# Banded values a step later in one row with scores and flips, warm-up matmuls at the start, and the last tile in halves

## The reference, cut to what matters

```python
hn = rmsnorm(x, norm_g[l])
proj = hn @ w_in[l]                       # 1024 -> 3072
u, g_main, q_mem, g_mem = jnp.split(proj, [D_MAIN, 2 * D_MAIN, 2 * D_MAIN + D_MEMW], axis=-1)
if l < N_A:   # layer 0: causal conv and RG-LRU recurrence on u
    y = rglru(causal_conv(u, ...))
else:         # layer 1: rope(u) are the queries of a sliding-window attention with sinks
    y = sink_attend(rope(u), k_att, v_att, band_mask, sinks)   # 16 heads, window 128
om = mem_attend(q_mem, mem_k[l], mem_v[l])                     # 4 heads, 256 memory rows
z = concat([y * silu(g_main), om * silu(g_mem)])
x = x + z @ w_out[l]                      # 1536 -> 1024
```

## Time and profile before

| what | value |
|---|---|
| three runs | 2111.63 to 2113.28 us, median 2112.22 us |
| the profiled execution's own time | 2113.13 us |
| its span | 2111.3 us |
| TensorE matmuls busy | 2087.1 us, 99% |
| VectorE busy | 1148.6 us, 54% |
| ScalarE busy | 923.7 us, 44% |
| granted TensorE clock over the span | 0.999 |

### The profile page before, as it was taken

The page is one execution under the profiler, slowest core; times in us unless marked ns, Lnnn a source line. Parts: engine busy times, 40 slices in busy tenths (PEclk is TensorE's granted clock), DMA queues, the critical chain, the costliest instruction groups (busy, mean ns, idle before and its releaser), DMA issues.

```text
span 2111.3 us, 29268 instructions
## 1 busy us (share of the span) xinstructions
PE 2087.1 (99%) x11869; PEld 1676.5 (79%) x11869; DVE 1148.6 (54%) x2015; ACT 923.7 (44%) x2012; POOL 26.8 (1%) x30
## 2 busy tenths in 40 slices
PE   7999999999999999999999999999999999999998
PEld 6888887777777788788788888888888888787886
DVE  4845446777776822221635444676777777723232
ACT  5733335777777723222534333444434445422111
POOL 0000000000000000000400000000000000000000
PEclk9999999999999999999999999999999999999999
DMA  9311111111111465343111111212222214475353
GB/s 388 127 63 45 63 49 54 45 50 44 44 49 63 164 214 180 107 125 101 61 43 43 36 43 48 78 52 79 69 71 78 68 54 135 132 269 188 89 192 104
DMA packets 116159, 206.28 MB, mean 98 GB/s; under 512 B 12349, under 2 KB 66941, under 8 KB 111025
## 3 DMA queue, kind: packets, MB, share of 16 engines
q1 hardware_dynamic: 116024, 204.42, 28.9%
HBM read 155.97 MB, written 48.48 MB: 97 GB/s over the span
## 4 chain that ended last, share of the span: by engine, by line
PE 92%; DVE 5%; ACT 2%; DMA 1%; issue 0%; SPq 0%; DVEq 0%
PE bank L569 49%; PE bank L1993 23%; PE bank L414 3%; PE bank L1132 3%; PE bank L674 2%; PE bank L1121 2%; PE bank L867 1%; PE bank L661 1%; PE bank L1102 1%; PE bank L649 1%; PE bank L589 1%; DVE wo_lo L1729 1%; PE bank L664 1%; PE bank L1981 1%; PE bank L1445 0%; DMA sm_rows<-srow_scratch 0%
## 5 line engine op out<-in xcount | busy, mean ns | idle before, releaser
L569 PE MATMUL bank<-x_hi,w_hi 128*128 128x512 f32 x1600 | 636.2, 398 | 1.2 <-ACT it_kraw L619 1.2
L569 PE MATMUL bank<-x_hi,w_lo 128*128 128x512 f32 x1600 | 624.1, 390 | 0.0
L569 PE MATMUL bank<-x_lo,w_hi 128*128 128x512 f32 x1600 | 623.3, 390 | 0.0
L569 PEld LDWEIGHTS bank<-x_hi,w_hi 128*128 128x128 f32 x1600 | 300.2, 188 | 100.7 <-issue 39.4
L569 PEld LDWEIGHTS bank<-x_hi,w_lo 128*128 128x128 f32 x1600 | 300.3, 188 | 64.4
L569 PEld LDWEIGHTS bank<-x_lo,w_hi 128*128 128x128 f32 x1600 | 300.5, 188 | 60.7 <-issue 0.7
L1993 PE MATMUL bank<-wo_hi,z_hi 128*128 128x512 f32 x768 | 303.1, 395 | 2.1 <-DVE z_lo L1758 2.1
L1993 PE MATMUL bank<-wo_hi,z_lo 128*128 128x512 f32 x768 | 299.2, 390 | 0.0
L1993 PE MATMUL bank<-wo_lo,z_hi 128*128 128x512 f32 x768 | 299.1, 389 | 0.0
L1168 ACT ACTIVATE it_X<-it_X,stat 128x128 f32<-128x128 f32 x256 | 99.2, 389 | 172.7 <-DVE stat L1238 172.7
L1993 PEld LDWEIGHTS bank<-wo_hi,z_hi 128*128 128x128 f32 x768 | 144.2, 188 | 35.3 <-DVE z_lo L1758 3.2
(11 more groups left out here) (311 smaller groups left out, 2649.6 us busy)
## 6 DMA issues: line engine op xcount, KB each, us to landing
w_raw<-in_w_items SPq DMA_DIRECT2D x25, 1024.0 KB, 5.1
z_scratch<-it_gz SPq DMA_DIRECT2D x96, 256.0 KB, 2.4
z_raw<-z_scratch SPq DMA_DIRECT2D x32, 768.0 KB, 5.7
it_cs<-in_rope SPq DMA_DIRECT2D x32, 512.0 KB, 4.1
wo_raw<-in_w_out SPq DMA_DIRECT2D x6, 2048.0 KB, 9.0
mk_w<-in_w_mem_kv SPq DMA_DIRECT2D x8, 1024.0 KB, 7.0
in_rows<-in_x_prompt SPq DMA_DIRECT2D x4, 2048.0 KB, 28.5
in_x<-in_x_T SPq DMA_DIRECT2D x4, 2048.0 KB, 25.4
```

The lines of the kernel that those rows point to most:

```text
L569: last = nc.tensor.matmul(ps, s_, r_, start=(k == 0 and q == 0), stop=(k == KT - 1 and q == 2))
```

## The change

At the start the memory rows and the first weight block are loaded in halves, 18 matmuls on a tile of ones (`WARM`) stand ahead of `memory(pe, 0)`, and the small sums and spreads stand later. In the banded attention `swa_values` of chunks 0 to 27 (LATE = 28) moves from the end of step q+2 to the middle of step q+3, ahead of the scores, and the flips move behind the scores; the samples' projection moves to q % 4 = 1, between values and scores. The last item's four chunks keep their step for the values. On VectorE `swa_result` of chunks 0 to 27 moves with them, to the head of step q+3, ahead of `swa_weights`. At the end the samples' tile becomes the last but one, and the last prompt tile is normalised and stored in halves.

```diff
+WARM = 18
...
+        s.dma_start(mt[:, half(0), 0:M], A["mem_T"][:, half(0)]).then_inc(mm_ld0, 16)
+        s.dma_start(w[0][:, half(0), :], A["w_mem_kv"][0][:, half(0)]).then_inc(first_half, 16)
+        s.dma_start(mt[:, half(1), 0:M], A["mem_T"][:, half(1)]).then_inc(mm_ld, 16)
+        s.dma_start(w[0][:, half(1), :], A["w_mem_kv"][0][:, half(1)]).then_inc(mk_ld[0], 16)
         s.dma_start(mt[:, :, M:NM], A["xs_T"]).then_inc(mm_ld, 16)
-        load_w(0)
...
+        act.wait_ge(ids, 2)
+        nc.scalar.activation(st[:, 63:64], m.eps, ACT.Copy)
         act.wait_ge(prm_ld, 16)
+        act.wait_ge(mm_ld0, 16)
+        memory_gain(0, range(0, 4))
         act.wait_ge(mm_ld, 32)
-        memory_gain(0)
+        memory_gain(0, range(4, KT))
...
         pe.wait_ge(ids, 1)
+
+        for i in range(WARM):
+            nc.tensor.matmul(m.bank[7][:, 0:128], ones[:, :], ones[:, :], start=True, stop=True)
         memory(pe, 0)
+        memory(pe, 1)
         memory_sums()
-        memory(pe, 1)
-        memory_spread()
         spread(pe, 0)
         memory(pe, 2)
+        memory_spread()
         memory(pe, 3)
...
     NQ = NCH * 2 * NP
+    LATE = NQ - NCH
...
+
+            if 0 <= q - 3 < LATE:
+                swa_values(pe, q - 3)
+            if q < NQ and q % 4 == 1:
+                of_samples(project_samples, pe, "main", *ipc(q)[:2])
+            if 1 <= q <= NQ:
+                swa_scores(pe, q - 1)
             if q >= 2:
                 swa_flip(pe, q - 2)
-            if 1 <= q <= NQ:
-                swa_scores(pe, q - 1)
...
-            if q >= 2:
+            if q - 2 >= LATE:
                 swa_values(pe, q - 2)
-            if q < NQ and q % 4 == 0:
-                of_samples(project_samples, pe, "main", *ipc(q)[:2])
...
             ahead["ahead_of_dve"](v, q)
+            if 0 <= q - 3 < LATE:
+                swa_result(v, q - 3)
             if q >= 2:
                 swa_weights(v, q - 2)
...
-            if q >= 2:
+            if q - 2 >= LATE:
                 swa_result(v, q - 2)
...
+
+    SAMPLES = TT - l
+    tokens = lambda t: t if t < SAMPLES else t - 1
+    rows = lambda t: NS if t == SAMPLES else 128
...
+    def last_square(act):
+        t, p = TT, TT % 2
+        act.wait_ge(sx[p], t_0 + 16 * (t // 2))
+        for h in range(2):
+            e = slice(512 * h, 512 * h + 512)
+            act.wait_ge(xn, 2 * na + 2 * t + h + 1)
+            nc.scalar.activation(y_of(t)[:, e], x_of(t)[:, e], ACT.Square, accum_out=st[:, 6 + h:7 + h]).then_inc(ss, 1)
+        act.wait_ge(ss, 2 * na + 2 * t + 2)
+        nc.scalar.activation(st[:, 2 + p:3 + p], st[:, 7:8], ACT.Sqrt, bias=st[:, 8:9], scale=1.0 / D).then_inc(ss, 1)
+
+    def last_rows(v, c):
+        t, p = TT, TT % 2
+        v.wait_ge(ss, 2 * na + 2 * t + 1)
+        c.link(nc.vector.tensor_scalar(st[:, 8:9], st[:, 6:7], 1.0 / D, EPS, ALU.mult, ALU.add))
+        v.wait_ge(mmd, halves_at(t, 1))
+        x = x_of(t)[:, 512:1024]
+        nc.vector.tensor_tensor(x, x, bank(t, 1), ALU.add).then_inc(xn, 1)
+        v.wait_ge(ss, 2 * na + 2 * t + 3)
+        c.link(nc.vector.reciprocal(st[:, 4 + p:5 + p], st[:, 2 + p:3 + p]))
+        for h in range(2):
+            e = slice(512 * h, 512 * h + 512)
+            nc.vector.scalar_tensor_tensor(y_of(t)[:, e], x_of(t)[:, e], st[:, 4 + p:5 + p], fg[:, e], ALU.mult, ALU.mult).then_inc(yn, 1)
...
-        for t in range(TT):
+        for t in range(TT + l):
+            if l == 1 and t == SAMPLES:
+                samples_raw(pe)
+                continue
```

More of the change, by code:

```diff
@@ L404, in memory @@
         l = i // 4
-        pe.wait_ge(mk_ld[i], 16)
+        if i:
+            pe.wait_ge(mk_ld[i], 32 if i == 4 else 16)
         if i >= 4:
@@ L409, in memory @@
             for k in range(KT):
+                if i == 0 and h == 0 and k % 4 == 0:
+                    pe.wait_ge((first_half, mk_ld[0])[k // 4], 16)
                 if h == 0 and i % 4 == 0:
@@ L1180, in swa_act @@
                 evac_branch(act, "main", *ipc(q), qraw[:, :], SWA_SCALE)
+            if q < NQ and q % 4 == 1:
+                of_samples(evac_samples, act, "main", *ipc(q)[:2])
             if 1 <= q <= NQ:
@@ L1193, in swa_act @@
                 weights_act(act, item("main", *ipc(q)[:2]) + 1, halves[q % 4])
-            if q < NQ and q % 4 == 0:
-                of_samples(evac_samples, act, "main", *ipc(q)[:2])
     def swa_weights(v, q):
@@ L1301, in swa_sp @@
             ahead["late_sp"](s, q)
-            if q >= 2:
+            if 0 <= q - 3 < LATE:
+                store_z(s, "main", *ipc(q - 3))
+            if q - 2 >= LATE:
                 store_z(s, "main", *ipc(q - 2))
-            if q < NQ and q % 4 == 0:
+            if q < NQ and q % 4 == 1:
                 of_samples(store_samples, s, "main", *ipc(q)[:2])
@@ L1696, in output @@
     st = m.stat
-    rows = lambda t: 128 if t < TT else NS
+    SAMPLES = TT - l
+    tokens = lambda t: t if t < SAMPLES else t - 1
+    rows = lambda t: NS if t == SAMPLES else 128
     slot = lambda t: (t + l) % 2
@@ L1702, in output @@
     xsrc = lambda t: ((A["x_prompt"][0, t * 128:(t + 1) * 128, :] if t < TT else A["x_sample"].rearrange("b s d -> (b s) d")) if l == 0
-                      else m.x1_d[t * 128:t * 128 + rows(t), :])
+                      else m.x1_d[TT * 128:TA, :] if t == SAMPLES else m.x1_d[tokens(t) * 128:tokens(t) * 128 + 128, :])
     xdst = lambda t: (m.x1_d[t * 128:t * 128 + rows(t), :] if l == 0
-                      else (outs["y_p"][0, t * 128:(t + 1) * 128, :] if t < TT else outs["y_s"].rearrange("b s d -> (b s) d")))
+                      else outs["y_s"].rearrange("b s d -> (b s) d") if t == SAMPLES else outs["y_p"][0, tokens(t) * 128:tokens(t) * 128 + 128, :])
     tiles_at = lambda i: [t for t in range(TT + 1) if place(t) == i]
@@ L1860, in sync @@
             if l == 1:
-                s.wait_ge(yn, na + t + 1)
-                s.dma_start(xdst(t), y_of(t)[0:rows(t), :]).then_inc(sx[t % 2], 16)
-            if l == 1 and 9 <= t <= 14:
-                k = 2 * (t - 9)
+                for e in ([slice(0, D)] if t < TT else [slice(0, 512), slice(512, D)]):
+                    s.wait_ge(yn, na + t + 1 + (e.start > 0))
+                    s.dma_start(xdst(t)[:, e], y_of(t)[0:rows(t), e]).then_inc(sx[t % 2], 16)
+            if l == 1 and 8 <= t <= 13:
+                k = 2 * (t - 8)
                 s.wait_ge(sm["zs_r"], sm["zs_0"] + 3)
@@ L1870, in stored @@
         for i in range(3 if l == 0 else 2):
-            s.wait_ge(sx[i], t_0 + 16 * len(tiles_at(i)))
+            s.wait_ge(sx[i], t_0 + 16 * (len(tiles_at(i)) + (l == 1 and i == place(TT))))
     def flipped(act, u):
@@ L1921, in scalar @@
             n, p = rows(t), t % 2
+            if l == 1 and t == TT:
+                last_square(act)
+                continue
             act.wait_ge(xn, 2 * na + 2 * (t + 1))
@@ L1945, in vector @@
                 x = x_of(t)[0:n, h * 512:(h + 1) * 512]
-                b, o = (bank(t, h), 0) if t < TT or l == 0 else (bank(t, 0), 32 * h)
-                if t == TT:
+                b, o = (bank(t, h), 0) if t != SAMPLES or l == 0 else (bank(t, 0), 32 * h)
+                if t == SAMPLES:
                     d = 32 if l == 0 else 64
@@ L1950, in vector @@
                 nc.vector.tensor_tensor(x, x, b[o:o + n, :], ALU.add).then_inc(xn, 1)
+                if l == 1 and t == TT:
+                    last_rows(v, c)
+                    return
             v.wait_ge(ss, 2 * na + 2 * t + 2)
@@ L1986, in product @@
         wh, wl = (w[:, k, h * 512:(h + 1) * 512] for w in (m.wo_hi, m.wo_lo))
-        if t < TT:
-            a, b = (z[slot(t)][:, k, :] for z in (m.z_hi, m.z_lo))
+        if t != SAMPLES:
+            a, b = (z[slot(tokens(t))][:, k, :] for z in (m.z_hi, m.z_lo))
             pairs = ((a, wh), (a, wl), (b, wh))
@@ L1992, in product @@
         for q, (s_, r_) in enumerate(pairs):
-            last = nc.tensor.matmul(bank(t, h)[0:128 if t < TT else 40, :], s_, r_, start=(first and q == 0), stop=(end and q == len(pairs) - 1))
+            last = nc.tensor.matmul(bank(t, h)[0:128 if t != SAMPLES else 40, :], s_, r_, start=(first and q == 0), stop=(end and q == len(pairs) - 1))
         return last
@@ L2010, in half @@
         if h == 0:
-            if t < TT:
-                pe.wait_ge(zlo, nt + t + 1)
-            else:
-                pe.wait_ge(sm["zs_r"], sm["zs_0"] + 3)
+            pe.wait_ge(zlo, nt + tokens(t) + 1)
         if t == 1 and h == 0:
@@ L2037, in samples_raw @@
                 j = 64 * (k % 2) + 32 * h
-                last = nc.tensor.matmul(bank(TT, 0)[j:j + 32, :], sm["z2"][:, k, :], w_again[:, k, h * 512:(h + 1) * 512], start=(k < 2), stop=(k >= NI - 2))
+                last = nc.tensor.matmul(bank(SAMPLES, 0)[j:j + 32, :], sm["z2"][:, k, :], w_again[:, k, h * 512:(h + 1) * 512], start=(k < 2), stop=(k >= NI - 2))
                 if k == NI - 1:
@@ L2042, in tensor @@
     def tensor(pe, done):
```

(7 more changed lines are left out.)

11 lines of the change are left out of this document (5 added, 6 removed).

## The result

The changed kernel took 2133.56 us, median of five runs (2132.06 to 2135.55). The ratio to the kernel before is 1.010, with a 95% interval of 1.0089 to 1.0111: slower by 1%. It runs 6.6 us above the predicted 2127 and 1.6 above the range's upper end. The profiled execution is the longest of the five: 2135.55 us, span 2133.8, which is 22.5 us above the span before; the sum had said 14.8.

A forecast was written before the change was run, and what follows sets the result against it. TensorE's matmuls, filling 99% of the span, were taken to bound the kernel before. Start -2.0, middle +17.4, behind it +1.5 and end -2.1 sum to +14.8 us, giving a median of 2127 us, range 2118 to 2132.

The forecast's parts named there:

- the sum: Whole kernel: start -2.0, middle +17.4, behind it +1.5, end -2.1, together +14.8 us.
- Direction and mechanism: Banded attention: two flips an item wait for `swa_result`, chance 0.72; slower by over 0.2%, chance 0.90.
- The rounds: VectorE's or TensorE's time per banded attention step, whichever decides: 17.53, 16.94, 15.35 and 16.33 us, an item of 66.15.
- the second rival: Banded attention: VectorE decides in every step, also those without `weights_low`, with waits at every flip; 2131 us, chance 0.18.
- The saving of tile changes: TensorE in the banded attention: fewer changes of tile shape save 0.25 us a step (0.2 to 0.3).
- The middle, +17.4: Banded attention: VectorE's longer rounds make it 17.4 us longer; bounds -7 and +3 for other cases.
- The uncovered piece: VectorE's round in the banded attention: result, release, eight flips and return, covered by nothing, add 1.87 us.
- The stalled interval outside the six items: Banded attention ahead of the six whole items: one interval, with `weights_low` in step 2, adds 1.4 us.
- The four last intervals save 0.25 each, -1.0: End of the banded attention, behind the six whole items: four steps each save 0.25 us, together -1.0.
- The start, -2.0: Up to the first projection: earlier loads and spread save 2.0 us, between -2.6 and -1.2 with a slow clock.
- Behind the middle, +1.5: First output projection product: TensorE, its scores now ahead of the flips, waits 1.5 us more for z_lo (0 to 1.7).
- The end, -2.1: From the last sample matmul to the span's end: shorter work after the matmuls saves 2.1 us (-1 to -2.6).

The follow-up runs named there:

- wait_filled: Changed kernel plus useless matmuls (8 or 5 of 512 columns) on TensorE in 13 steps, filling its wait ahead of the flips; 2130.41 us, ratio 1.0083.
- low_shadow: Changed kernel with `weights_low` of steps q % 4 = 1 and 2 moved right behind `swa_max` on VectorE; 2110.0 us, ratio 0.9988.
- low_gate: Changed kernel with `weights_low` moved behind `swa_max` and the gate product moved between `swa_result` and the masked weights, a step later; 2103.93 us, ratio 0.9962.
- cover_gone: `low_gate` with TensorE's row as scores, samples, values, flips, so nothing stands between values and flips; 2128.59 us, ratio 1.0077.
- after_again: The changed kernel unaltered, run once more for a second trace; 2132.20 us, ratio 1.0093.
- old_tail: `low_gate` with flips ahead of scores again in the steps from 31 on; 2104.49 us, ratio 0.996.
- ends_only: Changed kernel with the banded attention put back to its old order, start and end staying changed; 2109.19 us, ratio 0.9987.

## Why the prediction was right and wrong

**The step, by stretches.** Time from one step's first projection matmul to the next's, for steps 22 to 25, and the stretch of the middle:

| step | before | after | wait_filled | low_shadow | low_gate | cover_gone |
|---|---|---|---|---|---|---|
| 22, `weights_low` and first chunk | 15.58 | 17.58 | 17.61 | 16.02 | 15.41 | 16.20 |
| 23, `weights_low` | 15.58 | 17.02 | 16.99 | 15.41 | 15.31 | 16.20 |
| 24 (before: samples) | 16.58 | 15.42 | 15.41 | 15.40 | 15.31 | 16.20 |
| 25 (after: samples) | 15.57 | 16.31 | 16.31 | 16.31 | 16.31 | 17.19 |
| item | 63.31 | 66.33 | 66.32 | 63.14 | 62.34 | 65.79 |
| middle | 498.41 | 519.79 | 517.89 | 496.94 | 491.15 | 515.67 |

**Direction and mechanism: right.** The rounds were forecast as 17.53, 16.94, 15.35 and 16.33 us; they are 17.6, 17.0, 15.4 and 16.3. Thirteen flips wait for L651, 23.0 us in all, where 13 or 14 and some 23 were named; the steps without `weights_low` do not wait, which was the second rival's case. Undoing the middle, shortening VectorE's part and removing the cover each moved the time by what this mechanism asks.

**The saving of tile changes: right.** 0.25 us a step was forecast and 0.24 measured, once nothing else decides.

**The middle, +17.4: right in kind, mis-sized by 4.0 us.** The uncovered piece is 1.93 us and not 1.87, and it enters three rounds of an item: 0.18 more, six times, +1.1. The stalled interval outside the six items costs 1.7 and not 1.4, +0.3. "The four last intervals save 0.25 each, -1.0" was the weakest term: with the first three steps, all that lies outside gives back 0.3 us in place of 1.0, +0.7, since step 30 has the values of two chunks (17.98 against 15.58) and only the first three steps' missing values pay for it. The falls of the clock, +1.9 in this trace and 0.7 in the second, were not in the sum at all.

**The start, -2.0: this step failed.** In both traces of the changed kernel it is 0.0. The prediction let a slow clock cost at most 1.4 us, in block 0, with 1.2 us of slack behind it. The spread's slack was there (1.17 us of wait), but the clock fell behind it in one trace, and in the other it fell on top of a late second half of the rows. In the traces of the six other kernels that begin in the same way, the first projection is at 41.6 to 42.0, 1.4 to 1.9 us earlier, near the forecast value. Two of them (`low_shadow`, `cover_gone`) had a fall at 12.0 and 13.1 us, inside block 0, and lost nothing by it: there the slack did what the prediction said. So the gain exists in kernels with this start and is lost in some executions; that the changed kernel itself ever has it no trace shows. The bounds of this term, -1.2 to -2.6, should have held 0.

**Behind the middle, +1.5: the size near, the cause wrong.** It is +3.45 in this trace, of which 1.6 us are put down to a fall of the clock at 1829.9: without one the same stretch (303.37) takes 301.79 us in `wait_filled`; in `after_again` it takes 302.19, by which the fall would be 1.2. The wait for z_lo itself grew by 1.8 us (0.52 in the earlier trace rows, 2.29 now). The cause that was given, scores that now stand ahead of the flips so that TensorE arrives too early, explains 0.3 of it by `old_tail`.

**The end, -2.1: right** (-2.4 from the last matmul on, and `ends_only` pays 0.3 for the samples' product ahead of it).

In sum, against 14.8: start 2.0, item and edges 2.1, falls of the clock outside the start 3.5, z_lo 0.35, end -0.3 make 22.5 with rounding. Two thirds of the miss of 7.7 us, 5.2 us, are falls of the clock (1.7 in the start, 1.9, 1.6). This is the step that failed: the prediction gave TensorE waits of up to 2.2 us where it had had none, asked what the clock does for the start alone, and put it at nothing behind these waits. `wait_filled`, with these waits filled, had no fall and the start's gain, and at 2130.4 us lies inside the range. The range was also drawn wider downward than its terms: by the bounds given they end near 2119, not 2118. The Trainium skill (TensorE: Matmul & The Clock Gate, section HAM oscillation — how this bites in real kernels) describes this for waits on DMA in a loop: the clock falls in the wait and the work behind it is slow. The trace agrees in kind (granted clock 0.57 in the stretch behind the wait); here the waits are on another engine, and only the part of the slow work that this engine waits for costs time.

## What to carry to other kernels

When an exchange between two engines is moved, follow the bank: what stands between the instruction that fills it, the one that empties it and the one that fills it again, on both engines; here the same move of the values made the middle 7 us shorter or 21 longer, by what stood ahead of `swa_result` on VectorE, and 17 longer where TensorE's scores did not cover it. Before such a move, look for the wait that an engine spends idle on the way (3.2 us for the exponentials) and put work there that nobody waits for. And price a new wait of TensorE with what the clock may do behind it, but only for the instructions that the slower engine waits for.
